# Second routed block: two of four slot writes issued inside the plan; latent heads shared with GpSimd, rotary moves on two DMA queues

## The reference, cut to what matters

```python
q = (rms_norm(c_q, cq_norm) @ w_uq).reshape(B, S, H, dn + dr)
kv = (rms_norm(c_kv, ckv_norm) @ w_ukv).reshape(B, S, H, dn + dv)
k = jnp.concatenate([kv[..., :dn], broadcast(k_rope)], axis=-1);  v = kv[..., dn:]
q = rms_norm(q, q_norm);  k = rms_norm(k, k_norm)
q = jnp.concatenate([q[..., :dn], rope(q[..., dn:], pos)], axis=-1)
k = jnp.concatenate([k[..., :dn], rope(k[..., dn:], pos)], axis=-1)
```

```python
g_p, g_idx = lax.top_k(g_probs, 1)
e_p, e_idx = lax.top_k(jax.nn.softmax(e_logits, axis=-1), TOP_K)
hid = jax.nn.silu(einsum('td,edf->tef', t, w_gate)) * einsum('td,edf->tef', t, w_up)
y = jnp.einsum('tef,efd->td', hid * combine[..., None], w_down)
```

## Time and profile before

| | us |
|---|---|
| median of 3 runs | 2108.09 (2106.91 to 2111.71) |
| the profiled execution: its time | 2114.92 |
| its span | 2113.4 |
| TensorE busy | 2004.0 (95%) |
| VectorE, ScalarE, GpSimd busy | 1227.6 (58%), 940.3 (44%), 204.2 (10%) |
| mean granted TensorE clock | 0.985 |

### The profile page before, as it was taken

One profiled execution on the slowest core, in us unless ns is written; L12 is line 12 of the kernel. 1 busy time (PEld: TensorE's weight loads), 2 busy tenths in 40 slices (PEclk: granted clock), 3 DMA queues, 4 the chain that ended last, 5 costly groups with the idle time before them and its releaser, 6 DMA issues. The chain is left out here.

```text
span 2113.4 us, 32315 instructions
## 1 busy us (share of the span) xinstructions
PE 2004.0 (95%) x12489; PEld 1574.1 (74%) x12489; DVE 1227.6 (58%) x1672; ACT 940.3 (44%) x1219; POOL 204.2 (10%) x193
## 2 busy tenths in 40 slices
PE   7998889999999999998999999998999899988998
PEld 5865447888888888887888878786577578777776
DVE  3356476532333344547666566888368854547887
ACT  2125545532222331234656565775253633416774
POOL 0010100000000000004001110012112210003111
PEclk9999999999999999999999999999999999999999
DMA  9108024240442540117777887995320000248996
GB/s 250 38 21 306 14 60 130 60 135 26 120 125 60 184 160 1 50 42 237 278 271 273 283 283 274 393 392 233 89 80 30 13 1 1 81 177 235 387 384 231
DMA packets 221483, 338.62 MB, mean 160 GB/s; under 512 B 50421, under 2 KB 135573, under 8 KB 221374
## 3 DMA queue, kind: packets, MB, share of 16 engines
q1 hardware_dynamic: 214238, 316.78, 44.2%
q0 software_dynamic: 7136, 20.34, 2.6%
HBM read 309.07 MB, written 26.95 MB: 159 GB/s over the span
## 5 line engine op out<-in xcount | busy, mean ns | idle before, releaser
L1884 DVE TENSOR_TENSOR moe_pass_wL<-moe_pass_w,moe_pass_wH 128x2048 fp32r<-128x2048 f32 (+1 forms) x144 | 303.3, 2112 | 110.8 <-ACT moe_pass_wH L1805 110.7
L1805 ACT ACTIVATE moe_pass_wH<-moe_pass_w 128x2048 fp32r<-128x2048 f32 (+1 forms) x144 | 254.9, 1773 | 127.1 <-PE PS L652 86.0
L1884 DVE TENSOR_TENSOR hm_pass_wL<-hm_pass_w,hm_pass_wH 128x2048 fp32r<-128x2048 f32 x60 | 135.7, 2287 | 29.5 <-ACT hm_pass_wH L1805 29.4
L650 PE MATMUL PS<-moe_pass_wL,moe_pass_xgH 128*128 128x512 f32 (+1 forms) x384 | 147.8, 385 | 3.4 <-DVE moe_pass_wL L1884 2.1
L652 PE MATMUL PS<-moe_pass_wH,moe_pass_xgH 128*128 128x512 f32 (+1 forms) x384 | 143.2, 373 | 0.0
L651 PE MATMUL PS<-moe_pass_wH,moe_pass_xgL 128*128 128x512 f32 (+1 forms) x384 | 143.2, 373 | 0.0
L650 PE MATMUL PS<-xnT_low,ffn_upH 128*128 128x512 f32 (+2 forms) x360 | 138.9, 386 | 0.3 <-PE PS L652 0.3
L652 PE MATMUL PS<-ffn_xH,ffn_upH 128*128 128x512 f32 (+2 forms) x360 | 138.7, 385 | 0.0
L651 PE MATMUL PS<-ffn_xH,ffn_up_low 128*128 128x512 f32 (+2 forms) x360 | 138.7, 385 | 0.0
L1805 ACT ACTIVATE hm_pass_wH<-hm_pass_w 128x2048 fp32r<-128x2048 f32 x60 | 112.1, 1910 | 16.4 <-DMA hm_pass_w<-in_exp_w_up 7.0
L1110 DVE TENSOR_TENSOR ffn_hT<-ffn_sg,PS 128x512 f32<-128x512 f32 x22 | 15.1, 688 | 160.9 <-PE PS L652 160.9
(11 more groups left out here) (883 smaller groups left out, 4716.7 us busy)
## 6 DMA issues: line engine op xcount, KB each, us to landing
moe_pass_w<-in_moe_w_down SPq DMA_DIRECT2D x40, 1024.0 KB, 6.8
moe_pass_w<-in_moe_w_gate SPq DMA_DIRECT2D x32, 1024.0 KB, 7.1
moe_pass_w<-in_moe_w_up SPq DMA_DIRECT2D x32, 1024.0 KB, 8.1
hm_pass_w<-in_exp_w_gate SPq DMA_DIRECT2D x40, 512.0 KB, 7.5
hm_pass_w<-in_exp_w_up SPq DMA_DIRECT2D x40, 512.0 KB, 7.1
hm_pass_w<-in_exp_w_down SPq DMA_DIRECT2D x40, 512.0 KB, 7.3
od_W<-in_od_w_in SPq DMA_DIRECT2D x12, 1024.0 KB, 10.5
moe_pass_w<-in_moe_w_gate SPq DMA_DIRECT2D x16, 768.0 KB, 7.0
```

The lines of the kernel that those rows point to most:

```text
L650: nc.tensor.matmul(out, lh, rl, start=start, stop=False)
L1805: nc.scalar.activation(wH[:, i % S, 0:n], w[:, i % R, 0:n], ACT.Copy).then_inc(s["high"], 1)
L1884: nc.vector.tensor_tensor(wL[:, i % S, 0:n], w[:, i % R, 0:n], f32(wH[:, i % S, 0:n]), ALU.subtract) \
```

## The change

In the second routed block, slot writes 0 and 1 move from the start of `hm_pass` into `hm_plan`, behind the gather of the first rows, after `dests` is made. The semaphore of the writes now outlives both stages (`tiles.sorted`). The first routed block has `ahead` = 0: its writes stay where they are.

In the latent heads GpSimd takes 7 of the 16 plain multiplies (both heads of query pairs 2 and 3, both of key pair 3, one of key pair 2). As it has no access to PSUM, ScalarE first copies those spread results with the gain into `sq` (4 copies). The second four k moves go to ScalarE's DMA queue. TensorE makes the key spreads in the order 3, 2, 0, 1, and issues 28 `stay_busy` matmuls before them. VectorE's 1/root of the keys comes one query pair earlier.

```diff
@@ RouteTiles
+        self.sorted = new_semaphore(nc, name + "_sorted")
+        self.ahead = 0 if OVER else 2
+    def sort(self, pool, slots, c, t):
+        pool.indirect_dma_start(out=slots, out_offset=bass.IndirectOffsetOnAxis(ap=self.dests[:, c, t:t + 1], axis=0),
+                                in_=self.ids[:, t:t + 1], in_offset=None).then_inc(self.sorted, 16)
@@ plan_passes, gpsimd, behind the gathers
+            if tiles.ahead:
+                pool.wait_ge(s["destined"], 1)
+                for t in range(tiles.ahead):
+                    tiles.sort(nc.gpsimd, slots, 0, t)
@@ plan_passes, vector
-            nc.vector.tensor_copy(dests[:, :, :], at[:, :, :])
+            nc.vector.tensor_copy(dests[:, :, :], at[:, :, :]).then_inc(s["destined"], 1)
@@ sorted_passes, gpsimd
-                    nc.gpsimd.indirect_dma_start(...).then_inc(s["sorted"], 16)
-            pool.wait_ge(s["sorted"], 16 * NB * NT)
+                    if c or t >= tiles.ahead:
+                        tiles.sort(nc.gpsimd, C.slots[name], c, t)
+            pool.wait_ge(tiles.sorted, 16 * NB * NT)
@@ latent_heads
+        by_pool = [(qr, qm, 2, 0), (qr, qm, 2, 1), (qr, qm, 3, 0), (qr, qm, 3, 1), (kn, km, 3, 0), (kn, km, 3, 1), (kn, km, 2, 1)]
+        kept_at = (1, 1, 2, 2, 3, 3, 4)
@@ gpsimd, behind the memsets
+            for i, (src, dst, m, a) in enumerate(by_pool):
+                pool.wait_ge(s["spread_kept"], kept_at[i])
+                if dst is qm:
+                    pool.wait_ge(s["q_copied"], 4)
+                rows = slice(a * HD, (a + 1) * HD)
+                nc.gpsimd.tensor_tensor(dst[rows, 2 * m + a], src[rows, m], sq[rows, kept_at[i] - 1], ALU.mult).then_inc(s["multiplied"], 1)
+            pool.wait_ge(s["multiplied"], len(by_pool))
@@ sync: 8 q moves as before, then
+            sp.wait_ge(s["k_roped"], 1)
+            for j in range(4):
+                move(sp, km, ko, 0, j)
             sp.wait_ge(s["moved"], 16 * 16)
@@ tensor
+            pe.wait_ge(s["q_roped"], 2)
+            stay_busy(nc, C, 28, 0)
             pe.wait_ge(s["k_rstd"], 1)
-            pe.wait_ge(s["q_roped"], 1)
             spread_out(1, 4)
             spread_out(1, 5)
-            pe.wait_ge(s["q_roped"], 2)
+            spread_out(1, 3)
+            pe.wait_ge(s["q_done"], 2)
+            spread_out(1, 2)
+            pe.wait_ge(s["q_done"], 4)
             spread_out(1, 0)
-            for m in range(1, 4):
-                pe.wait_ge(s["q_done"], 2 * m)
-                spread_out(1, m)
-            pe.wait_ge(s["q_done"], 8)
+            pe.wait_ge(s["spread_kept"], 1)
+            spread_out(1, 1)
+            pe.wait_ge(s["spread_kept"], 2)
             value(1)
@@ scalar
+            def keep_spread(n, slot, i, rows=slice(0, P)):
+                act.wait_ge(s["made"], n + 1)
+                nc.scalar.activation(sq[rows, slot], PS[rows, n % 8, :], ACT.Copy, scale=gm[rows, 3 * i:3 * i + 1]).then_inc(s["spread_kept"], 1)
             power(15, 1)
-            for n, t in ((22, 0), (29, 1), (30, 2), (31, 3)):
+            keep_spread(20, 0, 0)
+            keep_spread(21, 1, 0)
+            take_v(22, 0)
+            keep_spread(25, 2, 1)
+            keep_spread(26, 3, 1, slice(HD, P))
+            act.wait_ge(s["k_roped"], 2)
+            for j in range(4):
+                move(act, km, ko, 1, j)
+            for n, t in ((29, 1), (30, 2), (31, 3)):
                 take_v(n, t)
@@ vector
-            for m in range(4):
-                nope(18 + m, 0, m, qr, qm, s["q_done"])
-                if m == 1:
-                    newton(15, 1, s["k_rstd"])
+            nope(18, 0, 0, qr, qm, s["q_done"])
+            newton(15, 1, s["k_rstd"])
+            nope(19, 0, 1, qr, qm, s["q_done"])
...
-            for m in range(4):
-                nope(25 + m, 1, m, kn, km, s["k_done"])
+            nope(27, 1, 0, kn, km, s["k_done"])
+            nope(28, 1, 1, kn, km, s["k_done"])
+            nope(26, 1, 2, kn, km, s["k_done"], (0,))
```

More of the change, by code:

```diff
@@ L1293, in plan_passes @@
 def plan_passes(nc, C, name, tiles, hits, token_rows, kept, pick, weigh, exps, busy, weights=None, token_weights=None, ring=None):
+    slots = C.slots[name.replace("plan", "pass")]
     Q, NC, NE, CAP, OVER, V = 16, len(hits), tiles.NE, tiles.CAP, tiles.OVER, tiles.V
@@ L1301, in sb @@
         return m.enter_context(sbuf(nc, name + n, shape, F32))
-    with ExitStack() as m2, stage(nc, name, "masked counted chosen placed hot last found indexed paired exped weighed weights_kept spread steps") as (block, s):
+    with ExitStack() as m2, stage(nc, name, "masked counted chosen placed hot destined last found indexed paired exped weighed weights_kept spread steps") as (block, s):
         mask, cnt, t, more = sb("_mask", [P, NT, NE], m2), sb("_cnt", [P, NE], m2), sb("_t", [P, 4, NE], m2), sb("_more", [P, NE, 4], m2)
@@ L2697, in latent_heads @@
     with ExitStack() as mem, stage(nc, "ev_latent_heads", "zeroed spread made squared q_copied k_copied q_cos k_cos k_sin k_turned q_sin "
[L2698 removed]
+                                   "q_turned logged exped steps q_rstd k_rstd q_roped k_roped q_done k_done v_taken moved "
+                                   "spread_kept multiplied") as (block, s):
         def sb(name, shape):
@@ L2716, in _ @@
                 step(nc.gpsimd.memset(t[ROT:HD].rearrange("p (j e) n -> p j e n", e=2)[:, :, 1], 0.0))
+            for i, (src, dst, m, a) in enumerate(by_pool):
[5 more added lines that the diff above has]
+            pool.wait_ge(s["multiplied"], len(by_pool))
         @block.sync
         def _(sp):
[L2720 to L2725, removed]
+            for e in range(2):
+                sp.wait_ge(s["q_roped"], e + 1)
+                for j in range(4):
+                    move(sp, qm, qo, e, j)
+            sp.wait_ge(s["k_roped"], 1)
+            for j in range(4):
+                move(sp, km, ko, 0, j)
             sp.wait_ge(s["moved"], 16 * 16)
@@ L2876, in gained, with nope @@
                 return nc.vector.scalar_tensor_tensor(out=dst, in0=src, scalar=gm[:, col:col + 1], in1=other_, op0=ALU.mult, op1=ALU.mult)
-            def nope(n, i, m, src, dst, done):
+            def nope(n, i, m, src, dst, done, heads=(0, 1)):
                 dve.wait_ge(s["made"], n + 1)
-                for a in range(2):
+                for a in heads:
                     rows = slice(a * HD, (a + 1) * HD)
```

12 lines of the change are left out of this document (7 added, 5 removed).

## The result

The changed kernel is **slower by 0.3%**: 2116.15 us (median of 13 runs, 2109.55 to 2120.35) against 2108.44 (13 runs, 2106.68 to 2111.72), ratio 1.0032 [1.0023, 1.0041]. Measured once more later beside its halves it came to 1.0014 [1.0002, 1.0025]. The forecast was 2100.2, with 2107.0 as its upper end.

What follows compares the result with a forecast made beforehand. TensorE, busy 95% of the span, was taken to bound the kernel. Gains of 5.3 us in the routed block and 2.6 in the latent heads, 7.9 together, off 2108.09 gave 2100.2; range 2097.5 to 2107.0.

Steps and rivals of the forecast that it cites:

- I take 0: Second routed block's plan: two slot writes behind the gather cost 0, up to 1 us if beside VectorE's large subtract.
- Rival 3: Plan: slow DMA stretch moves there, delaying the token weights 7.0 us, and the first pass's stop stays: 2112.5; chance 0.06.
- the lone write caused nothing: Argument against the slow stretch moving into the plan: the first slot write, at 1907 to 1911, met nothing.
- The first pass: Second routed block: TensorE's 3.57 us stop and 1.72 us of low clock both go, 5.3 us gained.
- a stop like item 7's may be smaller in others; I keep the differences: First pass: the profiled execution lies 6.8 us above the median, yet its gains are taken off 2108.09 unchanged.
- Rival 1: First pass: the slot writes don't hold the loads, or one is enough; routed block gains 0, 2105.5; chance 0.18.
- The rule of the Trainium skill: Routed block: queues take turns at packet boundaries, so 4-byte writes cost loads almost nothing and this half brings 0.
- The latent heads: Attention's first product starts at 292.9 instead of 295.54, with ScalarE last: 2.6 us gained.
- 1/root 3.3: Latent heads: VectorE's keys' 1/root still takes 3.3 us, so k_rstd is there at 283.1.
- Rival 2: Latent heads: GpSimd's multiplies slow beside VectorE and end the stage, 2101.6 or 2107.0; chance 0.10.
- The clock: Attention's first microseconds: no gain counted after a 2.4 us stop; at most 1.5 us.
- ScalarE's moves: Latent heads: four move issues of 0.59 us each end at 290.8, the last landing at about 292.2.

Runs made afterwards that it cites:

- heads_only: Kernel before with only the changed latent heads, slot writes as before: 2110.71 us, ratio 0.9995.
- heads_again: Kernel before with only the changed latent heads, measured once more: 2106.27 us, ratio 0.9988.
- wide_before: Kernel before with 64 bytes instead of 4 per slot in the second routed block, no writes moved: 2106.95 us, ratio 0.9988.
- apart_after: Changed kernel with slot writes still 4 bytes, but to places 64 bytes apart in the second routed block: 2108.80 us, ratio 0.9985.
- late_wide_hold: Changed kernel with 64-byte slots, the token weights' wait moved to GpSimd, and GpSimd's multiplies held until the keys' 1/root: 2102.68 us, ratio 0.9967.
- late_after: Changed kernel with the wait for the token weights moved from SyncE to GpSimd, behind its slot writes: 2106.32 us, ratio 0.9974.
- wide_after: Changed kernel with 64 bytes instead of 4 per slot in the second routed block: 2108.27 us, ratio 0.9993.
- late_before: Kernel before with the wait for the token weights moved from SyncE to GpSimd, behind the four slot writes: 2107.51 us, ratio 0.9986.
- after: The changed kernel itself, both halves, against the kernel before: 2116.15 us, ratio 1.0032.

## Why the prediction was wrong

**The step that failed: "I take 0" for the two early writes.** They took the time forecast, 1.02 and 0.97 us, right behind the gather, GpSimd had its cover, and its work ended at 1905.17 with the plan unmoved. The step priced them by GpSimd's time alone. What stood behind them was not GpSimd but the next DMA of another queue, the token weights, whose landing all engines wait for. It went from 2.2 to 8.7 us of waiting. TensorE's stop grew by 6.6 and the fillers behind it, at the low clock, by 1.5; the plan's end as a whole grew by 7.4 (23.11 less 15.71). The working looked at lengths of issue, not at landings. The earlier trace rows held the hint: the slot load came 13.91 us after the last write was issued, though 128 numbers of 4 bytes are nothing to carry.

**Rival 3 had the place and almost the price** (7.0 against 7.4, deciding from 2.6 on), but kept the stop in the first pass, and so ended at 2112.5; it had 0.06. What went is its second half: the stop did go. It was set against it that "the lone write caused nothing". That was the wrong evidence: the one write at 1907 to 1911 had no other transfer beside it whose landing anyone awaited.

**The first pass: right that the stop would go, the term too large.** The stop and the clock of 0.57 went, and the loads reached 378 GB/s from 8 us in. The pass became 36.50 - 32.12 = 4.4 shorter, not 5.3. And the profiled execution had the largest single stop, 3.57: `heads_only` and `heads_again` took 34.99 and 34.10 with the old writes, so the gain is 2 to 4.4, on the mean of the three 3.0. The sentence "a stop like item 7's may be smaller in others; I keep the differences" named the danger and didn't act on it. Over all executions without a late wait, the plan's end took 15.9 with the old writes (three) and 22.7 with the new (four): 6.8 lost and 3.0 won, 3.8 net. The runs with the slot writes alone have 1.7 and 3.0 (1.0008 and 1.0014), with intervals that hold 3.8. With the 0.9 of the heads taken off, 2.9 is left for the whole, which is its second measurement (1.0014).

**Rival 1** (the writes don't hold the loads) is out by `wide_before`: spacing the writes alone takes the stop away. The rule of the Trainium skill that was set against this half (turns at packet boundaries) didn't decide. The slot writes' own packets did take next to no time (0.6% of the engines' at 1922 to 1926), as the rule would have it; the loads' packets became slow beside them (140 at 92.5%, later 511 at 96.8%), of which the rule says nothing. Two other statements of the same page of the Trainium skill (DMA: Bandwidth & Descriptors) bear on this. In Queues, rings and completion order it says that an engine's semaphore increment is an ordered write that lands only after every earlier write of that DMA engine, across its queues. By that rule the token weights' semaphore waits for the slot writes' own completion, and the rows fit it: the packets gone by 1907, the second slot write's landing 7.8 us after its issue and the token weights' behind it, 9.1 after theirs, and back to a 2.2 us wait once the writes are spaced. In Specifications it says that below 512 bytes the engine does read-modify-write. That alone doesn't tell the runs apart, as the spaced writes are below 512 bytes too and were not slow. That neighbours in one stretch of DRAM wait for each other is our reading of `apart_after`; no run here shows the inside of it.

**The latent heads: the starting point right, two terms missed.** Predicted 2.6, measured about 0.9 over the executions: the heads took 22.37, 21.20, 22.89, 22.63 and 23.79 in those with the old function and no fillers (mean 22.6), and 21.4 or 22.3 in the eight with the new (mean 21.65). The terms:
- *1/root 3.3* became 6.7 (attention's start came 1.5 earlier instead of 2.6, 17.06 after `lh_qo` for 18.52), so k_rstd came at 286.5, not 283.1. Rival 2 had seen that the two engines would meet, but had it cost GpSimd (1.27 became 1.5 over the first four); the cost fell on VectorE: its steps with all operands in SBUF went from 0.68 to 1.18 and 1.64, the cast from 0.42 to 1.38, while the step that reads PSUM stayed at 0.68 and the key multiplies at 0.77. The Trainium skill (SBUF — State Buffer, Who interferes with whom) has it as an exclusive lock: a VectorE instruction with two SBUF inputs, or one in a two-port mode, and a GpSimd instruction that reads SBUF keep each other out for a whole instruction. The trace agrees on which steps are slowed: the three with two SBUF inputs (the prediction had counted two), and the cast if it runs in such a mode, which no run shows. That GpSimd is the cause is shown by `late_wide_hold`, where the hold alone brings 1/root back to 3.3. The rule speaks against this placement of GpSimd's work, and the prediction had looked for it only on GpSimd's side.
- *The clock*, counted as no gain and no loss. In the changed kernel the stop before attention is 2.75 us (2.4 forecast), and the twelve products took 5.46 where they had taken 4.06: a loss of 1.4, as large as what had been won. That pair was unlucky: on the mean they took 4.75 with the new heads (eight executions) and 4.24 with the old (five, 2.84 to 5.46), a loss of 0.5. 1.5 less 0.5 is the 0.9 measured.
- *ScalarE's moves* took 0.69 each (2.77 for four), not 0.59, from 289.39; the value copies 0.52, ending at 293.77, ScalarE last as forecast. GpSimd's multiply of 64 rows took 1.28, the 1.27 forecast.
- *Fillers* of 28 ended by 285.2, not 286.0, and cost nothing as k_rstd was later.

**The first routed block**: 0, as forecast.

## What to carry to other kernels

A small DMA costs what its landing delays, so before one is moved ahead, list every semaphore of any queue that is awaited behind it; here the landings took 9.1 to 11.0 us. Scattered words of 4 bytes close together in DRAM were slow to land and slowed the loads' packets and one landing behind them; 64 bytes of room for each took that away where moving them had only moved the cost. And GpSimd's help slowed the steps of VectorE that read two SBUF tensors, and not those that read PSUM: hold it back behind a chain that reads only SBUF, if it has the time. Fillers where TensorE would otherwise stand are worth a try; here they went with a full clock in both executions that had them, and one without had it too.

## What the runs showed of the hardware

- A DMA of 8 KB issued 1.3 us after the second of two slot writes landed 9.1 us after its issue (11.0 in `late_after`), with no packet moving for most of it. In the kernel before, without writes ahead of it, SyncE waited 2.2 us for the same landing; with the writes 64 bytes apart 2.2 us (`apart_after`) and 2.7 us (`wide_after`).
- The slot writes themselves landed 7.3, 11.5, 15.2 and 16.2 us after their issue to neighbouring words (`late_before`), and 2.2, 6.2, 6.3 and 6.0 with 64 bytes each (`wide_before`).
- Behind slot writes to neighbouring words the loads ran at 161 GB/s from 5 to 9 us into the pass (after), and at 28 in the earlier trace rows; with the same writes spaced, at 333 from 5 to 9 us. The engines' busy share was 0.93 at 127 GB/s and 0.98 at 378.
- The slot write's issue on GpSimd took 0.97 to 1.02 us, but 2.8 to 3.1 beside VectorE's large subtract of two SBUF tensors (128x2048), spaced or not, and 0.97 beside the one that reads PSUM (`heads_only`). Three long ones stand in the shortest first pass (`wide_before`).
- VectorE's SBUF steps beside GpSimd's multiplies: 0.68 became 1.18 and 1.64, 0.42 became 1.38.
- TensorE's clock ahead of attention: the twelve products took 2.84 (full clock) after stops of 1.48, 1.66 and 3.65, and 4.51 or 5.46 after stops of 2.73 to 2.75 (late_after, after). A shorter stop did not go with a higher clock throughout.
